# First block's attention: scores with keys on the partitions, and row maxima taken from products of rounded operands

## The reference

```
h = rms_norm(x, n1) * (1 + sc1) + sh1
a_b, a_c, a_h, b_v, b_g, c_q, c_k, c_v, d_q, d_k, d_v = split_proj(h @ w_in)
...
ya = short_conv_mixer(a_b, a_c, a_h, conv_a)
yb = conformer_conv(b_v, b_g, conv_b, conv_b_bias, cln_g, cln_b)
yc = window_attention(apply_rope(q_heads(c_q), cos, sin), apply_rope(kv_heads(c_k), cos, sin),
                      kv_heads(c_v), kc_c, vc_c, sink)
yd = global_attention(apply_rope(rms_norm(q_heads(d_q), qn_g), cos, sin), ..., kc_d, vc_d)
x_new = x + g1 * (jnp.concatenate([ya, yb, yc, yd], axis=-1) @ w_out)
```

## Time and profile before

| what | value |
|---|---|
| median of 3 runs | 3902.67 us (3902.58 to 3907.64) |
| the profiled execution, its own time | 3902.73 us |
| its span, first to last instruction | 3900.9 us |
| mean granted TensorE clock | 0.86 |
| TensorE busy | 3302.3 us, 85% |
| VectorE, ScalarE, GpSimd busy | 1055.7, 659.3, 440.3 us |

### The profile page before, as it was taken

One profiled execution on the slowest core, in us unless ns is written; L12 is line 12 of the kernel. 1 busy time (PEld: TensorE's weight loads), 2 busy tenths in 40 slices (PEclk: granted clock), 3 DMA queues, 4 the chain that ended last, 5 costly groups with the idle time before them and its releaser, 6 DMA issues. The chain is left out here.

```text
span 3900.9 us, 41076 instructions
## 1 busy us (share of the span) xinstructions
PE 3302.3 (85%) x16972; PEld 1921.7 (49%) x16972; DVE 1055.7 (27%) x2000; ACT 659.3 (17%) x1275; POOL 440.3 (11%) x636
## 2 busy tenths in 40 slices
PE   3799998479999938999758777479998998879997
PEld 0456773323333303577332111168785586748875
DVE  0225542321111122443130000132324266222232
ACT  0111120100000111111100000032222155122231
POOL 1006700011111110170001111100000000000000
PEclk7896558589999968855869999889999979989998
DMA  9131000369999891100249999912312100132130
GB/s 393 39 97 44 1 0 11 140 234 389 385 388 391 308 374 54 65 1 1 78 172 413 414 412 412 371 54 87 108 58 97 65 1 1 65 113 87 65 119 27
DMA packets 141428, 637.02 MB, mean 163 GB/s; under 512 B 11824, under 2 KB 19008, under 8 KB 86000
## 3 DMA queue, kind: packets, MB, share of 16 engines
q1 hardware_dynamic: 121104, 575.58, 37.4%
q0 software_dynamic: 20192, 59.58, 5.0%
HBM read 611.95 MB, written 23.17 MB: 163 GB/s over the span
## 5 line engine op out<-in xcount | busy, mean ns | idle before, releaser
L897 PE MATMUL bank<-slots,HT 128*32 128x512 f32 x4096 | 479.1, 600 | 79.3 <-DMA slots<-in_w_up_dram 41.5
L667 PE MATMUL bank<-slots,HT 128*128 128x512 f32 (+2 forms) x960 | 400.7, 578 | 20.4 <-ACT done_mark L1531 20.4
L897 PEld LDWEIGHTS bank<-slots,HT 128*32 128x32 f32 x4096 | 121.7, 110 | 400.8 <-issue 243.4
L667 PEld LDWEIGHTS bank<-slots,HT 128*128 128x128 f32 x960 | 182.4, 192 | 230.3 <-issue 204.5
L667 PE MATMUL bank<-hT_high,chunk_high 128*128 128x512 f32 x704 | 277.3, 394 | 8.3 <-DVE low_slots L1922 8.3
L667 PE MATMUL bank<-hT_high,low_slots 128*128 128x512 f32 x704 | 277.7, 395 | 0.0
L667 PE MATMUL bank<-hT_low,chunk_high 128*128 128x512 f32 x704 | 276.9, 393 | 0.0
L916 PE MATMUL bank<-arena,HT 128*32 128x512 f32 x2048 | 243.9, 596 | 26.7 <-DMA arena<-in_w_down_dram 26.2
L698 PE MATMUL bank<-ident,arena 128*128 128x128 f32 x272 | 61.0, 402 | 223.0 <-DVE arena L1593 145.5
L667 PE MATMUL bank<-HT,slots 128*128 128x512 f32 (+1 forms) x480 | 172.3, 521 | 1.7 <-ACT done_mark L1531 1.7
L698 PEld LDWEIGHTS bank<-ident,arena 128*128 128x128 f32 x272 | 50.2, 212 | 237.5 <-issue 198.8
(11 more groups left out here) (323 smaller groups left out, 4431.0 us busy)
## 6 DMA issues: line engine op xcount, KB each, us to landing
slots<-in_w_gate_dram SPq DMA_DIRECT2D x128, 1024.0 KB, 8.6
slots<-in_w_up_dram SPq DMA_DIRECT2D x128, 1024.0 KB, 11.0
arena<-in_w_down_dram SPq DMA_DIRECT2D x128, 1024.0 KB, 13.2
slots<-in_ada_w_dram SPq DMA_DIRECT2D x24, 2048.0 KB, 22.2
slots<-in_w_in_dram SPq DMA_DIRECT2D x15, 2048.0 KB, 13.0
slots<-in_ffn_w_gate_dram SPq DMA_DIRECT2D x10, 2048.0 KB, 8.5
slots<-in_ffn_w_up_dram SPq DMA_DIRECT2D x10, 2048.0 KB, 8.8
slots<-in_ffn_w_down_dram SPq DMA_DIRECT2D x10, 2048.0 KB, 7.8
```

The lines of the kernel that those rows point to most:

```text
L667: mm = pe.matmul(out_, lhsT, rhs, start=(n == 0), stop=(n == len(pairs) - 1))
L897: mm = pe.matmul(bank[32 * j:32 * j + 32, 2 + n, :], xT[:, kk0 + kk, lo:lo + 32], w[n][:, kk, 512 * h:512 * h + 512], start=(pair == 0 and ...
```

## The change

The order of the attention is turned round. The work is now in groups of one `kind` and one key/value head `g` (two query heads, `j` = 0 and 1): in layer 0 four groups for the context and then four for the tokens, in layer 1 only the latter; in each set both `kind` 1 groups come first. A group goes over its key tiles. In a step, TensorE computes the scores with 128 keys as the stationary operand and up to 512 queries as the moving one, so that the result already has the keys on the partitions (`scores`, L883, L890, L893). ScalarE takes the exponential of all of it in one instruction per head (L1436), and TensorE multiplies it, 512 columns at a time, with the values as stationary operand (`mix`, L911). Beside the 64 value columns stand 64 columns of ones, so that the same product gives the sums. Nothing is turned any more.

The maxima must be known ahead of the exponential, and a maximum over keys is now one over partitions. So queries and keys get a 65th row: in the keys it is 1, in the queries minus the maximum of that query's scores, and the product subtracts it. The maxima come from a second set of scores in the old orientation (`row_scores`), made from copies of both operands rounded to float32r (`round_operands` on ScalarE, L1414 and L1415). VectorE reduces them (L1895, L1897), TensorE turns the columns of maxima into rows (`turn_shift`, L870), and ScalarE puts them in place (`take_shift`, L1406 and L1408). This runs two groups ahead of the scores in layer 0 and one group ahead in layer 1. The end of a group: ScalarE copies sums and values out of the banks (`take_outcome`, L1427 and L1428), VectorE takes the reciprocal of the sums over 512 columns and multiplies (`outcome`, L1936 and L1938).

Other edits: ScalarE's copies in `qkv` are split by head (L1369, L1370, L1382); GpSimd writes the constant rows at the start of `qkv`; GpSimd computes the 31 taps first and the 3 taps after, with products four deep; the extended queries live in the slots of the `w_out` weights and the rounded copies in those of the `qkv` weights, so SP loads the `w_out` weights only after the last product of the attention, and the first expert pieces behind them.

```diff
@@ SyncE
+                if stage.name == "attend":
+                    attended = stage.at("mixed", stage.signals["mixed"])
+                if stage.name == "w_out":
+                    sp.wait_ge(sem["mixed"], attended)
@@ TensorE, attend
-                n = len(units)
-                for i in range(n + 3):
-                    if i < n:
-                        scores(i)
-                    if 1 <= i <= n:
-                        turn_probs(i - 1)
-                    if 2 <= i <= n + 1:
-                        mix(i - 2)
-                    if i >= 3 and (i - 3) % HEADS == HEADS - 1:
-                        turn_y((i - 3) // HEADS)
+                ahead = 2 if st.layer == 0 else 1
+                for group in groups[:ahead]:
+                    rows_of(group)
+                    turn_shift(group)
+                scores(groups[0].steps[0])
+                for group in groups:
+                    later = groups[group.number + ahead] if group.number + ahead < len(groups) else None
+                    units = list(later.units) if later else []
+                    share = -(-len(units) // (len(group.steps) - 1))
+                    for n, one in enumerate(group.steps):
+                        if n + 1 < len(group.steps):
+                            scores(group.steps[n + 1])
+                            for unit in units[share * n:share * n + 1]:
+                                row_scores(unit)
+                        else:
+                            if later:
+                                turn_shift(later)
+                            if group.number + 1 < len(groups):
+                                scores(groups[group.number + 1].steps[0])
+                        mix(one)
+                        if n + 1 < len(group.steps):
+                            for unit in units[share * n + 1:share * n + share]:
+                                row_scores(unit)
@@ VectorE, attend
-                    if i < n:
-                        maximum(i)
-                    if 1 <= i <= n:
-                        take_probs(i - 1)
-                    if i < TAPS_B:
-                        tap(i)
-                    if i >= 2 and (i - 2) % HEADS == HEADS - 1:
-                        rows_of_y((i - 2) // HEADS)
+                for group in groups:
+                    if group.number + ahead < len(groups):
+                        for unit in groups[group.number + ahead].units:
+                            maximum(unit)
+                            tap_some(1)
+                    else:
+                        tap_some(14)
+                    outcome(group)
+                tap_some(3 * TAPS_B)
@@ ScalarE, attend
+                for group in groups:
+                    for n, one in enumerate(group.steps):
+                        exponentials(one)
+                        if n == 0 and group.number:
+                            take_outcome(groups[group.number - 1])
+                        if n == 1 and to_round:
+                            round_operands(to_round.pop(0))
+                    if group.number + ahead < len(groups):
+                        take_shift(groups[group.number + ahead])
+                take_outcome(groups[-1])
```

More of the change, by code:

```diff
@@ L118, in place_stages, with __init__ @@
     return total
[L121 to L134, removed]
+class Group:
+    def __init__(self, number, kind, g, main):
+        self.number, self.kind, self.g, self.main = number, kind, g, main
+        self.queries = (0, SEQ) if main else (SEQ, NTOK)
+        self.heads = 2 * g
+        self.tiles = list(range(ST)) if main else list(range(ST, ST + CT))
+        self.keys = list(range(ST, ST + CT)) + (list(range(ST)) if main else [])
+        self.units, self.steps = [], []
@@ new lines, in local_tiles, with attention_plan @@
+def local_tiles(qt, kind):
+    return list(range(ST)) if kind else list(range(max(0, qt - 1), min(ST, qt + 2)))
+def attention_plan(layer):
+    kinds = [(kind, g) for kind in (1, 0) for g in range(2)]
+    order = ([(kind, g, False) for kind, g in kinds] if layer == 0 else []) + [(kind, g, True) for kind, g in kinds]
+    groups, units, steps, events = [], 0, 0, 0
+    last, taken = {}, {}
+    ahead = 2 if layer == 0 else 1
+    for number, (kind, g, main) in enumerate(order):
+        group = Group(number, kind, g, main)
+        for qt in group.tiles:
+            for j in (range(2) if main else [None]):
+                unit = Unit(units, group, qt, j)
+                if number < ahead:
+                    unit.pair = (4, 0, 2, 6)[units % 4]
+                unit.previous = taken.get(unit.pair)
+                taken[unit.pair] = units
+                group.units.append(unit)
+                units += 1
+        for kt in group.keys:
+            step = ScoreStep(steps, group, kt)
+            steps += 1
+            step.parts = []
+            for j in (range(2) if main else [None]):
+                b = 2 * (step.number % 2) + (j or 0)
+                step.parts.append((j, b, events, last.get(b)))
+                last[b] = events
+                events += 1
+            group.steps.append(step)
+        groups.append(group)
+    return groups, units, events
@@ L739, in attend @@
             def attend(st):
[L740 to L753, removed]
+                groups = st.facts["groups"]
@@ L760, in scores @@
                                 pe.matmul(scores_of_tile, ident[:, :], band[:, 0 if t < qt else 1, :], start=False, stop=True)
[L761 to L772, removed]
-                        for c in range(4, n):
-                            mm = pe.transpose(bank[:, 5, tile_cols(c - 4)], probs[:, i % 2, tile_cols(c)], ident[:, :])
-                        mm.then_inc(sem["full5"], 1)
@@ new lines, in exponentials @@
+                def exponentials(one):
+                    for j, b, event, previous in one.parts:
+                        act.wait_ge(sem["score_full"], st.at("score_full", event + 1))
+                        wait_read(previous)
+                        n = one.hi - one.lo if one.group.main else SEQ
+                        act.activation(probT[:, b, 0:n], bank[:, b, 0:n], ACT.Exp, scale=HD ** -0.5).then_inc(sem["prob_ready"], 1)
+                reads, mixes = {}, {}
+                read = mixed = 0
```

411 lines of the change are left out of this document (283 added, 128 removed).

## The result

| | before | after |
|---|---|---|
| median (lowest to highest) | 3905.15 us (3902.58 to 3908.72) | 3854.7 us (3850.52 to 3870.97) |
| profiled execution | 3902.73 us | 3870.97 us |

The ratio is 0.9878, 95% interval 0.9847 to 0.9909: faster by 1.2%, some 50 us. I had forecast 141 us, and 3854.7 is outside the range of 3715 to 3815. The rows of the profiled execution show where the other two thirds went.

The account below looks back on a forecast made before the run. TensorE, busy at 1.2 GHz throughout both attention stages, was taken to bound them. From 3902.7 us, minus 66 (layer 0) and 79.5 (layer 1), plus 4.5 (`qkv` copies), came 3761.7 us; range 3715 to 3815 for 8 in 10.

Parts of the forecast that it names:

- The other edits: Edits outside TensorE's attention steps: ScalarE's copies cost 4.5 us in all; GpSimd's fills and tap order nothing; `w_out` loads hidden.
- another engine ends the stage: Rival for attention: GpSimd would set layer 0's end only if contention made it a third slower; under 10 us, chance 3%.
- 13 + 23 + 52: Layer 0 before the token groups: opening 13 us, context groups 0 and 1 23 us, context groups 2 and 3 52 us.
- group 4: Layer 0's first token group, carrying window row units: 29.7 us, including 2.5 us for starting at the cold clock.
- the window groups and the tail: End of layer 0's attention: groups 6 and 7, without row units, 39.4 us, then last copies, reciprocal, multiply and finish 6.5 us.
- The clock rises to 2.4 GHz and falls for some microseconds at borders: TensorE in attention: 2.4 GHz after some 5 us of dense steps, 1.2 GHz again after a wait of some 4 us.
- The first two rivals: Attention clock stays at 1.2 GHz: 3931 us, chance 7%; window groups stay cold, 3841 us, or borders alone, 3805, chance 15%.
- Borders: Before the second row unit of groups 5 (layer 0), 1 and 2 (layer 1), TensorE waits about 4 us for VectorE.
- Placing the shift: At layer 1's group borders TensorE waits for ScalarE: 1.4 us, or 2.8 where two sink exponentials come first.
- ScalarE's copies at the end of `qkv`: Eight small copies instead of two, plus one more of the values, on the path before attention: 2.2 us more per layer.
- `w_out` waits for no transfer: The later-issued `w_out` weights need 9.1 to 12 us, hidden by the 6.5 us tail and `conv_out`; no cost.
- The page's clock line: Reading of the old profile: TensorE's clock sinks to 5 or 6 tenths twice, in slices 5 to 7 and 18 to 19.

Follow-up runs that it names:

- the kernel with a gap in each pair: The changed kernel, with GpSimd's 31-tap part waiting for each addition to finish before issuing the next product: 3773.3 us, ratio 0.9666.

## Why the prediction was wrong

**The step that failed** is one clause of "The other edits": "GpSimd's order of taps costs nothing as long as the stage lasts longer than its work". The stage lasted longer, and the order cost 104 us of 3871 in the profiled execution (78 us by the medians, 3854.7 against 3776.6 with the order turned back). I had taken contention as a price for each instruction (1.20 us a tap against 0.74), from a kernel in which VectorE came every 5 to 8 us. The change made two things at once: it put 67 us of GpSimd work without a gap at the head of the stage, where the 3-tap parts with their waits had been, and it thinned VectorE's requests there to tiny negations and, in layer 0, a first tap 21 us in. Neither alone does harm: the old attention with the new stream gives 1.0002, the new attention with the order turned back 0.967 to 0.972. Together, in the changed kernel, they let an instruction wait for the end of the stream. The rival "another engine ends the stage" had contention in it, but as a third more on each of GpSimd's instructions, "price under 10 us", at 3%. It should have asked what happens when GpSimd leaves no gap at all.

**The rest, by its own steps,** can be read from the kernel with a gap in each pair. Its stages begin and end here, with the first scores of groups 4, 5 and 6 of layer 0 between (timeline of TensorE):

```profile
328.04 1.22 PE L846 MATMUL bank<-arena,slots 65*128 65x256 f32 x2 [1.75 <-ACT done_mark L1723]
...
413.81 3.62 PE L890 MATMUL bank<-slots,arena 65*128 65x512 f32 x4
...
448.76 1.88 PE L890 MATMUL bank<-slots,arena 65*128 65x512 f32 x4
...
482.81 1.88 PE L890 MATMUL bank<-slots,arena 65*128 65x512 f32 x4
...
530.54 1.19 PE L753 MATMUL bank<-HT,mean_of 128*128 128x512 f32 x1 [5.91 <-issue]
...
1579.94 0.77 PE L854 MATMUL bank<-k_round,q_round 65*128 65x512 f32 x1 [3.02 <-ACT q_round L1415]
...
1724.44 1.19 PE L753 MATMUL bank<-HT,mean_of 128*128 128x512 f32 x1 [5.91 <-issue]
```

- Layer 0 takes 202.5 us (forecast 197.3), layer 1 144.5 (141.8): 8 us over in 339. In layer 0 the part up to the first wide scores takes 85.8 us (13 + 23 + 52 = 88 forecast), group 4 takes 35.0 (29.7) and group 5 34.1 (33.7), each up to the next group's first scores, the window groups and the tail 47.7 (45.9). So the total isn't met by large errors that cancel.
- *The clock rises to 2.4 GHz and falls for some microseconds at borders*: right in kind. Windows from 469 to 486 and 488 to 506 us have TensorE busy throughout at clock 1.00, and at the border to group 5 it is at 0.50 for 7 us. The first two rivals are out. But "after some 5 us of dense steps" was too early for group 4: TensorE is busy throughout from 413.8 us on, and its clock is 0.50 until 429 us (windows below). So 15 us ran at half the clock and not 5, which is the 5 us that group 4 is over.
- *Borders*: TensorE waits 3.09 us at 504.54 in the changed kernel ahead of the window units of group 5, and 2.38 and 2.44 us at 1737.38 and 1773.30; I had 4.
- *Placing the shift* in layer 1: 1.1 and 2.24 us, forecast 1.4 and 2.8.
- *ScalarE's copies at the end of `qkv`* in layer 0: from the last turning to the first product of the attention 3.3 us pass in the changed kernel (327.51 to 330.81) and 2.2 before (324.27 to 326.48), so 1.1 us more; I had 2.2. That the attention starts 4.3 us later than before is for the most part older: the last turning itself is 3.2 us late there, and 0.5 us late with a gap in each pair (324.75), whose stages are the same up to then.
- *`w_out` waits for no transfer*: right. Its first products, at 597.29 and 1842.49, wait for ScalarE's mark.
- *The page's clock line*: the first attention is slices 4 to 6, not 5 to 7, and slices 8, 15 and 21 sink to 5 or 6 as well. No term of the sum rests on this reading.

```profile
504.54 0.44 PE L858 MATMUL bank<-k_round,q_round 65*128 65x128 f32 x2 [3.09 <-DVE small L1895]
...
597.29 1.22 PE L753 MATMUL bank<-slots,HT 128*128 128x512 f32 x1 [9.04 <-ACT done_mark L1723]
```

These two lines are of the changed kernel. The windows are of the kernel with a gap in each pair:

```profile
425.00:428.00 3.00, 3.00 (x7) 1.45 (x6) 1.35 (x2) 0.00 (x0) 2.84 (x5) 0.50 0.03 5
428.00:431.00 3.00, 3.00 (x11) 1.65 (x10) 1.27 (x2) 0.54 (x1) 2.84 (x5) 0.80 0.00 0
431.00:434.00 3.00, 3.00 (x17) 1.92 (x15) 1.73 (x2) 0.66 (x2) 2.84 (x5) 1.00 0.00 0
```

## What to carry to other kernels

When two engines share a way to memory, don't cost the contention from a mean over a stage in which they alternate. Look at how long one of them runs without a gap, and at how long the other is quiet before it asks; if both grow, put a wait for its own last result into the dense stream, every few instructions (0.08 us each here; every fourth pair, 8.9 us, was enough), and look in the new trace for the longest single instruction of each engine. A single gap near the start wasn't enough: 3853.4 us with it after addition 0, 3788.3 after addition 2. A total of busy time (VectorE 29% of the span, before 27%) doesn't show a hang; the group's mean of one does.

## What the runs showed of the hardware

A GpSimd stream of float32 products and additions, back to back, kept out some VectorE instructions from memory to memory for up to 57.3 us, some 50 of its instructions long. This happened to scalar_tensor_tensor (a 128x4 as well as a 128x512), to tensor_tensor beside the stream's instructions of 256 columns, and to tensor_scalar of 128x512. Not all kinds were held up: VectorE's maxima over PSUM columns (the accumulation memory) ran beside the same stream at 0.69 and 0.95 us, and 20 reciprocals of 128x512 from memory to memory took 3.35 us beside it, as they did without it. All 20 hangs of the 18 traces ended at the first gap of the stream, of 0.08 or 0.14 us: each was done 0.02 to 0.56 us after that gap began.

The Trainium skill (SBUF — State Buffer, "Terms") says that the pair of ports for which both engines arbitrate is locked exclusively and held for the full instruction. Boundaries at which VectorE was let in agree with that (GpSimd's next instruction 1.46 instead of 1.03 us). The hangs don't follow from it: the sentence doesn't say who comes next, and if it were the engine that waits, the longest wait would be one instruction, 1.25 us in these rows.

What stays open is what decides whether a request hangs. That the time since the last gap plays a part is supported from both sides, with a gap that was moved and with taps that were moved: none of 812 requests hung under 9 us and all 13 from 16.7 to 23.7. But in between it isn't the later requests that hung, and nearly the same request hung in one kernel and passed in another, so something that these traces don't show decides too. A delay of VectorE's request against GpSimd's boundaries was not tried. What is shown is narrower: the dense stream causes the hangs, any gap ends one, and a gap at least every 8.9 us left none.
